# A two-block layer on one NeuronCore: u from x times g, the norm factor applied later, SSM parameters and shares in other places and types, norm sums in PSUM

## The reference, cut to what matters

```python
n = rmsnorm(h, g_mix)                    # h * rsqrt(mean(h*h) + eps) * g
z = n @ w_in                             # q, k, v of 12 heads; u (512 wide); two gates
# attention in three dilated groups of 4 heads, each with output o_g and log-denominator l_g
wts = softmax(stack(lses), axis=0)       # the "shares" of the three groups, per head and token
attn = sum(wts[..., None] * stack(outs))
y = gelu(s5_ssm(u, a_re, a_im, log_dt, b, c, d_skip))   # complex diagonal scan over u
h = h + (gate_a * (attn @ w_p) + gate_s * glu(y)) @ w_out
...                                      # norm n2, gated FFN
h = h + sigmoid(h @ w_ple_gate) * (p @ w_ple_proj)
return rmsnorm(h, g_final)               # and the second block begins with norm1 of this
# second block: adaptive norms, RG-LRU, latent attention, out projection, norm2, FFN, final norm
```

## Time and profile before

| | us |
|---|---|
| median of 3 runs | 1928.42 (1926.65 to 1929.37) |
| profiled execution | 1931.13 |
| its span, first to last instruction | 1929.3 |
| PE busy | 1859.4 (96%) |
| DVE busy | 1051.3 (54%) |
| ACT busy | 748.1 (39%) |
| POOL busy | 260.2 (13%) |

### The profile page before, as it was taken

The page is one execution under the profiler, slowest core; times in us unless marked ns, Lnnn a source line. Parts: engine busy times, 40 slices in busy tenths (PEclk is TensorE's granted clock), DMA queues, the critical chain, the costliest instruction groups (busy, mean ns, idle before and its releaser), DMA issues.

```text
span 1929.3 us, 20889 instructions
## 1 busy us (share of the span) xinstructions
PE 1859.4 (96%) x8140; PEld 1452.8 (75%) x8140; DVE 1051.3 (54%) x1562; ACT 748.1 (39%) x1181; POOL 260.2 (13%) x351
## 2 busy tenths in 40 slices
PE   5999999999999999999989999899999899999997
PEld 4888888777877888888867777666667688888885
DVE  7555454454556544553467594455545466435543
ACT  4454454442344222222343553345444244324431
POOL 7644551100000000000001140211110000000000
PEclk9999999989999999999989999999999899999998
DMA  4322222214334545552323223312104223332321
GB/s 170 115 67 88 87 67 91 88 56 142 98 124 164 178 162 187 185 184 87 126 66 115 82 67 104 125 33 72 44 22 160 86 77 89 97 99 90 96 87 56
DMA packets 64186, 199.31 MB, mean 103 GB/s; under 512 B 7124, under 2 KB 11476, under 8 KB 64088
## 3 DMA queue, kind: packets, MB, share of 16 engines
q1 hardware_dynamic: 64088, 197.97, 31.6%
HBM read 189.55 MB, written 8.39 MB: 103 GB/s over the span
## 4 chain that ended last, share of the span: by engine, by line
PE 70%; issue 20%; DVE 7%; ACT 2%; DMA 0%; POOL 0%; POOLq 0%; DVEq 0%; SPq 0%; ACTq 0%
PE bank L248 20%; PE bank L250 19%; PE bank L249 19%; PE bank L597 2%; PE bank L623 2%; PE bank L610 1%; PE bank L505 1%; DVE tile L1776 1%; DVE tiler L1307 1%; PE bank L277 1%; PE bank L317 1%; PE bank L333 1%; DVE wlo L1280 1%; ACT whi L753 1%; PE bank L395 1%
## 5 line engine op out<-in xcount | busy, mean ns | idle before, releaser
L248 PE MATMUL bank<-tiler,whi 128*128 128x512 f32 x2272 | 923.6, 407 | 15.1 <-DVE tiler L1307 5.3
L249 PE MATMUL bank<-tiler,whi 128*128 128x512 f32 x2272 | 902.7, 397 | 0.0
L250 PE MATMUL bank<-tiler,wlo 128*128 128x512 f32 x2272 | 902.5, 397 | 0.0
L753 ACT ACTIVATE whi<-raw 128x1024 fp32r<-128x1024 f32 x286 | 301.1, 1055 | 654.9 <-PE bank L250 649.3
L248 PEld LDWEIGHTS bank<-tiler,whi 128*128 128x128 f32 x2272 | 432.1, 190 | 139.1 <-issue 28.9
L250 PEld LDWEIGHTS bank<-tiler,wlo 128*128 128x128 f32 x2272 | 431.7, 190 | 101.8
L1280 DVE TENSOR_TENSOR wlo<-raw,whi 128x1024 fp32r<-128x1024 f32 x267 | 334.5, 1257 | 315.8 <-ACT whi L753 315.6
L249 PEld LDWEIGHTS bank<-tiler,whi 128*128 128x128 f32 x2272 | 432.4, 190 | 96.7 <-issue 2.9
L2016 POOL TENSOR_TENSOR stat<-stat,scl 128x4 f32<-128x4 f32 x7 | 7.9, 1130 | 1162.0 <-DVE stat L1298 725.8
L1954 DVE SCALAR_TENSOR_TENSOR tile<-bank,sm,tile 128x511 f32<-128x511 f32 x44 | 33.0, 750 | 98.4 <-ACT tile L1254 61.9
L2007 POOL TENSOR_TENSOR wlo<-raw,whi 128x1024 fp32r<-128x1024 f32 x19 | 45.5, 2397 | 257.9 <-ACT whi L753 257.9
(11 more groups left out here) (341 smaller groups left out, 1573.1 us busy)
## 6 DMA issues: line engine op xcount, KB each, us to landing
raw<-wst SPq DMA_DIRECT2D x286, 512.0 KB, 3.6
wide<-wadaT SPq DMA_DIRECT2D x48, 512.0 KB, 3.5
tile<-xT SPq DMA_DIRECT2D x16, 256.0 KB, 5.2
spare<-tile SPq DMA_DIRECT2D x16, 256.0 KB, 2.0
tile<-spare SPq DMA_DIRECT2D x16, 256.0 KB, 5.5
out<-tile SPq DMA_DIRECT2D x8, 256.0 KB, 2.0
tile<-gblk SPq DMA_DIRECT2D x5, 256.0 KB, 4.7
us<-tile SPq DMA_DIRECT2D x4, 256.0 KB, 4.7
```

Source lines behind the costliest of these rows:

```text
L248: e.matmul(bank, whi[:, o:o + 128], hi, start=start, stop=False)
L249: e.matmul(bank, whi[:, o:o + 128], lo, start=False, stop=False)
L250: e.matmul(bank, wlo[:, o:o + 128], hi, start=False, stop=stop).then_inc(*sig("blk", n))
L753: e.activation(whi[:, c % NHL * W:(c % NHL + 1) * W], raw[:, c % NRAW * W:(c % NRAW + 1) * W], ACT.Copy).then_inc(*sig("hi", c))
```

## The change

- **u from x times g.** ScalarE and VectorE make the two parts of x * g as soon as a tile of x is there (tiles `XG`), and TensorE makes all four u projections from them at once, k by k, in banks 4 to 7. The sum of n1 stands behind k = 4, the spread behind k = 5. The factor is copied to `RBS`, and `u_out` multiplies with it as u leaves the banks, on VectorE. Nine f32 matmuls on ones stand at the very start. q and k of head 0 are made side by side from the norm's operands, and the SP queue loads weight chunks between the tiles of x.
- **Order of the parameters.** The decay is made on VectorE in turn 0, the inputs in turn 1, the powers of the step in turn 2. The SSM's phases are one turn later, gelu and the parts of y too (turn 16). The root of n1 stands behind the low powers on GpSimd.
- **Shares in fp32r.** The weights are split into a high part (rows 0 to 3) and a low part (rows 32 to 35) of a tile that GpSimd has set to zero, and one fp32r matmul on 64 rows spreads their sum. The matrix that selects the row is loaded earlier and copied by ScalarE.
- **Sums in PSUM.** For r1 and r12 (PLE), n3 and the last norm the eighth square is no longer added by VectorE: `total2` sums the first seven, `total3` adds the sum over the eighth into the same four columns. `busy` puts f32 matmuls of ones of 128 columns around them. At the PLE gate ScalarE makes the squares of m - 1 ahead of the sigmoid of m.

```diff
+            def total2(name, acc, bank):
+                e.wait_ge(*at("acc", name, 6))
+                for j in range(4):
+                    e.matmul(bank[:, j:j + 1], F(acc)[:, j * 128:(j + 1) * 128], ones[:, 0:1], start=j == 0, stop=False,
+                             skip_group_check=True)
+
+            def total3(name, tmp, bank):
+                e.wait_ge(*at("sq", name, 7))
+                for j in range(4):
+                    ins = e.matmul(bank[:, j:j + 1], F(tmp)[:, j * 128:(j + 1) * 128], ones[:, 0:1], start=False, stop=True,
+                                   skip_group_check=True)
+                ins.then_inc(*sig("tot", name))
+
+            def busy(bank, n):
+                for _ in range(n):
+                    e.matmul(bank[:, 128:256], ones[:, :], ones[:, :], start=True, stop=True)
...
-            total("n1", 59, B[6])
-            spread("n1", 60, B[7])
-
-            proj2("in", 36, B[0], "in", 37, B[1], N1, "n1")
-            for j in (2, 3):
-                e.wait_ge(*at("u", j - 2))
-                proj("in", 36 + j, B[j - 2], N1)
+            for _ in range(9):
+                e.matmul(B[7][:, 0:128], ones[:, :], ones[:, :], start=True, stop=True)
+
+
+            for k in range(8):
+                e.wait_ge(*at("oplo", "xg", k))
+                for j in range(4):
+                    proj("in", 36 + j, B[4 + j], XG, [k])
+                if k == 4:
+                    total("n1", 59, B[2])
+                if k == 5:
+                    spread("n1", 60, B[3])
...
-                    e.wait_ge(*at("selp"))
+                    e.wait_ge(*at("sel_r"))
                 for g in range(3):
                     if h:
                         e.wait_ge(*at("omul", h - 1, g))
-                    e.matmul(B[2 + g], F(SELP)[0:4, h * 128:(h + 1) * 128], F(ROWS[0][g])[0:4, :], start=True,
-                             stop=True).then_inc(*sig("bc", h, g))
+                    e.matmul(B[2 + g], R(SELR)[0:64, h * 128:(h + 1) * 128], R(SHARE[g])[0:64, :], start=True, stop=True).then_inc(*sig("bc", h, g))
...
-                j, phase = (a - 2) // 3, (a - 2) % 3
+                j, phase = (a - 3) // 3, (a - 3) % 3
...
+                    if a == 0 and part < 2:
+                        if part == 0:
+                            proj2("in", 0, B[0], "in", 12, B[1], N1, "n1")
+                        continue
...
-            total("r1", 51, B[4])
-            total("r12", 52, B[5])
+            busy(B[6], 8)
+            total2("r1", 51, B[4])
+            total2("r12", 52, B[5])
+            total3("r1", 56, B[4])
+            total3("r12", 58, B[5])
+            busy(B[6], 10)
             spread("r12", 53, B[6])
             spread("r1", 54, B[7])
+            busy(B[4], 5)
...
-            total("n3", 24, B[6])
+            busy(B[7], 5)
+            total2("n3", 24, B[6])
+            total3("n3", 26, B[6])
+            busy(B[7], 8)
             spread("n3", 25, B[7])
+            busy(B[6], 9)
...
             e.activation(F(PP)[:, 0:16], col("ldt", 0, 16), ACT.Exp).then_inc(*sig("dt"))
-            for k in range(8):
-                e.wait_ge(*at("io%d" % k, 0))
-                square("n1", k, F(X_RAW[k]), 59, (60, 61))
-            e.wait_ge(*at("ang", 0))
-            e.activation(F(PP)[:, 80:96], F(PP)[:, 48:64], ACT.Sin).then_inc(*sig("sin", 0))
-            e.wait_ge(*at("ang", 1))
-            e.activation(F(PP)[:, 96:112], F(PP)[:, 64:80], ACT.Sin).then_inc(*sig("cos", 0))
-            prep(-CB)
+            prep(-2 * CB)
+            for k in range(9):
+                if k < 8:
+                    e.wait_ge(*at("io%d" % k, 0))
+                    e.activation(R(XG[k][0]), F(X_RAW[k]), ACT.Copy, scale=col("g_mix", k)).then_inc(*sig("ophi", "xg", k))
+                if k == 1:
+                    e.wait_ge(*at("ang", 0))
+                    e.activation(F(PP)[:, 80:96], F(PP)[:, 48:64], ACT.Sin).then_inc(*sig("sin", 0))
+                    e.wait_ge(*at("ang", 1))
+                    e.activation(F(PP)[:, 96:112], F(PP)[:, 64:80], ACT.Sin).then_inc(*sig("cos", 0))
+                if k in (2, 4):
+                    prep(4 * k - 2 * CB)
+                if k:
+                    square("n1", k - 1, F(X_RAW[k - 1]), 59, (60, 61))
+            prep(CB)
...
-                if a in (5, 8, 11, 14):
-                    ssm_y((a - 5) // 3)
+                if a in (6, 9, 12, 15):
+                    ssm_y((a - 6) // 3)
...
+                if a == 14:
+                    e.wait_ge(*at("selp"))
+                    e.activation(R(SELR)[0:64, :], F(SELP)[0:64, :], ACT.Copy).then_inc(*sig("sel_r"))
                 if a == 15:
                     attn_hi(0)
+                if a == 16:
                     for y in range(4):
                         e.wait_ge(*at("yt", y))
                         e.activation(F(U[y]).rearrange("p (c r) -> p r c", r=4), F(YJ[y]).rearrange("p (r c) -> p r c", r=4),
@@ -904,7 +949,6 @@
                     for y in range(4):
                         e.wait_ge(*at("gelu", y))
                         e.activation(R(Y_OP[y][0]), F(U[y]), ACT.Copy).then_inc(*sig("ophi", "y", y))
-                if a == 16:
                     attn_hi(3)
...
-                e.wait_ge(*made("pg", m))
-                if m >= 2:
-                    e.wait_ge(*at("h_pg", m - 2))
-                e.activation(F(SILU[m % 2]), B[m % 4], ACT.Sigmoid).then_inc(*sig("pg_s", m))
                 if m:
                     sums(m - 1)
+                e.wait_ge(*made("pg", m))
+                e.activation(F(SILU[m % 2]), B[m % 4], ACT.Sigmoid).then_inc(*sig("pg_s", m))
             prep(first.get(("in2", 0), 0))
...
-            e.wait_ge(*at("sq", "n1", 0))
-            for k in range(1, 8):
-                add_up("n1", k, 59, (60, 61))
-            variance("n1", B[6], 1024, ST_1)
             prep(-2 * CB)
+            for k in range(8):
+                hi, lo = XG[k]
+                e.wait_ge(*at("ophi", "xg", k))
+                e.scalar_tensor_tensor(out=R(lo), in0=F(X_RAW[k]), scalar=col("g_mix", k), in1=R(hi).bitcast(F32), op0=MUL,
+                                       op1=SUB).then_inc(*sig("oplo", "xg", k))
+                if k in (2, 4):
+                    prep(4 * k - 2 * CB)
+                if k >= 2:
+                    add_up("n1", k - 1, 59, (60, 61))
+            add_up("n1", 7, 59, (60, 61))
+            prep(CB)
+            variance("n1", B[2], 1024, ST_1)
             e.wait_ge(*at("ident"))
             diagonal("n1", ST_1, 60)
-            prep(-CB)
-            scaled("n1", 8, X_RAW, lambda k: col("g_mix", k), B[7], (62, 63, 65), N1)
+            scaled("n1", 8, X_RAW, lambda k: col("g_mix", k), B[3], (62, 63, 65), N1)
...
+            def u_out(j):
+                e.wait_ge(*made("in", 36 + j))
+                if j == 0:
+                    e.wait_ge(*at("rb_sb"))
+                e.tensor_tensor(F(U[j]).rearrange("p (r c) -> p c r", r=4), B[4 + j].rearrange("p (c r) -> p c r", r=4),
+                                F(RBS).rearrange("p (c r) -> p c r", r=4), MUL).then_inc(*sig("u", j))
+
+            u_out(0)
+            u_out(1)
+            start_of("in", 24)
...
+                then(ins)
+                e.wait_ge(*at("share0"))
+                for g in range(3):
+                    ins = e.tensor_copy(R(SHARE[g])[0:4, :], F(ROWS[0][g])[0:4, :])
+                then(ins)
+                for g in range(3):
+                    ins = e.tensor_tensor(R(SHARE[g])[32:36, :], F(ROWS[0][g])[0:4, :], R(SHARE[g])[0:4, :].bitcast(F32), SUB)
...
+                    if a == 0:
+                        u_out(2)
+                        u_out(3)
+                        decay()
...
-            e.wait_ge(*at("half"))
-            root("n1", ST_1)
...
             powers(lr, li, 4)
+            e.wait_ge(*at("half"))
+            root("n1", ST_1)
             powers(hr, hi_, 3)
...
             e.dma_start(sm[:, :], small[:, :]).then_inc(*sig("small", by=16))
+            chunks(1)
             for k in range(8):
                 e.dma_start(F(X_RAW[k]), xT[k]).then_inc(*sig("io%d" % k, 0, by=16))
+                if k in (2, 4):
+                    chunks(k // 2 + 1)
             e.dma_start(ident[:, :], consts[:, 0:128]).then_inc(*sig("ident", by=16))
```

204 lines of the change are left out of this document (108 added, 96 removed).

## The result

The changed kernel takes 1912.01 us (median of 4 runs, 1911.59 to 1913.66) against 1928.89 for the one before in the same set: ratio 0.9915, 95% interval 0.9898 to 0.9932, 16.9 us faster. The forecast was 1901, range 1891 to 1909: the direction is right, the size is not, and the time lies 3 us outside the range. The profiled execution took 1913.66, its span is 1911.9, 17.4 less than before.

A forecast was written before the change was run, and what follows sets the result against it. TensorE, busy 96% of the span, was taken as the bound. Gains 1.0 (start) + 14.5 (shares) - 1.2 (gelu) + 5 (PLE) + 5.1 (n3) + 3.1 (end) = 27.5 us off 1931.13 gave 1903.6, less 2.7: 1901, range 1891 to 1909.

The forecast's parts named there:

- The shares: Four share products per turn, fp32r instead of f32: 15.2 us saved, less a 0.7 stall for weights, gain 14.5.
- Gelu: Turn 16: gelu's work on ScalarE delays the gate of projection 53, which frees projection 55's bank: loss 1.2 us.
- The start: Up to head 0's scores: u's matmuls run while the first norm is made, GpSimd's root comes later; gain 1.0 us.
- PLE: Norm behind the PLE gate: sums in PSUM, earlier squares and a faster spread shorten the hole; gain 5 us.
- falling here leaves 3.6: PLE norm: if the clock falls during the one-column matmuls between the fillers, 3.6 us remain of a 6.3 gain.
- n3: Norm behind the second output projection: variance 2.6 us earlier, spread 1.2 shorter, 1.3 from faster matmuls behind; gain 5.1.
- End: Last norm: variance 1.9 us earlier and spread 1.2 shorter, gain 3.1; with a fallen clock 0.7.
- GpSimd runs nearly free: Rival, 17%: GpSimd's low powers are hardly hindered, factor at 28 to 30, start gains 8 to 10 us: 1893.
- shut out: Rival, 13%: dense vector work blocks GpSimd, 11 operations done by 22, the start loses 2 us: 1904.
- The fillers don't keep the clock up: Rival, 14%: the clock falls in the norms' holes despite fillers; they give 6.9 us, not 13.2: 1907.
- The shares stay slow: Rival, 4%: the fp32r share products don't speed up as meant, since half the rows count little; 6.8 us less: 1908.
- The SP queue behind u(3): Rival, 2%: writes of u waiting for u(3) hold chunk loads until the kernel is slower than before.

The follow-up runs named there:

- experiment 6: Changed kernel with the share products reading the f32 selector and f32 weights on 4 rows again, the weights' conversions left unused: 1924.71 us.
- experiment 2: Changed kernel with the four share groups one projection later on TensorE, last turn's SSM outputs ahead of the last combination on VectorE: 1906.59 us.
- experiment 8: Changed kernel with ScalarE's four copies behind the gelus and one attention copy moved behind the gate of projection 53: 1909.20 us.
- experiment 5: Changed kernel with the chunk's low part for head 0's values ahead of the sines, first two u products behind head 0's rotation: 1910.76 us.
- experiment 9: Changed kernel with ScalarE copying head 0's queries out of their bank ahead of the two sines instead of behind them: 1911.92 us.
- experiment 10: Changed kernel with the edits of experiment 5 and experiment 9 together: 1910.31 us.
- experiment 4: Changed kernel without the filler matmuls around the norms, the nine at the program's start kept: 1917.66 us.
- experiment 11: Changed kernel with n1's root amid the low powers, shares one projection later, mixed PLE fillers, chunk part and queries' copy ahead of the sines: 1897.68 us.
- experiment 12: Kernel of experiment 11 with two more chunk loads ahead of the writes of u on the SP queue: 1895.02 us.
- experiment 3: Changed kernel with four instead of eight fillers ahead of the PLE norm's sums and six between their pieces: 1911.30 us.

## Why the prediction was wrong in size

- **The shares, 14.5 forecast, 8.0 in the profile (the largest miss).** The step that failed is "the 24 matmuls of the last SSM block's output now stand ahead of the first share, 24 x 0.111 = 2.7". They stood ahead of it before as well, seventeen us earlier; timeline of TensorE, kernel before:

```profile
360.25 0.38 PE L371 MATMUL bank<-tile 128*128 128x128 f32 x2
```

  So TensorE is not later at the first share by their move: it would come at 379.8 as before, the weights were computed for 382.9, and 3.1 us of stall is the right sum, not 0.7 (2.95 measured). That stall brings a second price which I had named at 37.63 and did not add here: half clock behind it, 9.35 - 6.69 = 2.7 us (1.5 in seven other profiles with the same wait). And a share group costs 1.11, not 0.70, because each of its matmuls takes some 0.30 in place of 0.232 and the first projection matmul behind it 0.33: 1.6 over four. 14.5 - 2.3 - 2.7 - 1.6 = 7.9. The main mechanism, fp32r in place of f32, is right: experiment 6 takes it away, and experiment 2 takes away the stall and the half clock behind it.
- **Gelu, -1.2 forecast, -1.1 measured.** It is the wait at 425.52, at the gate that was named; experiment 8 removes it.
- **The start, +1.0 forecast, -0.6 in the profile.** Its parts came out nearly to the tenth: root at 33 (32.96), TensorE idle from 29, values' wait ended at 59 (59.37). The sum was short of the half clock behind that wait: from 59.37 to the scores it is 11.2 us for 36 matmuls, which take 8.4 at full clock; that is 2.9 for the clock where I added 1.6, and 0.4 comes from the later start. Five other profiles of kernels that are the same up to there have 69.21 to 70.15, so the typical gain is about 0.3. The count of GpSimd's operations rested on a poor pair of rows: the one of 1.26 us has 128 columns, which take 0.40 to 0.48 with nothing beside them, and the one of 0.21 has 16. The rule itself held: from 11.86 to 22 there are 17 operations of GpSimd and 14 of the vector engine. One cause I gave, the chunk part as the only gate, was wrong without harm: the queries' copy was the second (experiments 5, 9, 10).
- **PLE, 5 forecast, 2.0 in the profile.** Failed steps: "falling here leaves 3.6", which here left 2.0, because fillers at half clock cost double and then hold the spread by 1.1 us (I had priced them as free in every case); and "2.6 us of one-column matmuls", which are 3.5 at full clock (970.46 to 973.96 in experiment 2). In eight profiles with these fillers the hole is 11.70 (three), 13.1 to 13.2 (three) or 14.80 (two), where before it was 16.80: gains of 5.1, 3.6 and 2.0. The value of 5 is the good outcome, not the mean of 3.8. Without any filler one profile has 12.52 (experiment 4), so most of the gain here is not theirs. Timeline of TensorE in experiment 2 (11.70) and, last, in experiment 8 (13.17), where the clock fell among the ten fillers:

```profile
972.17 1.93 PE L281 MATMUL bank<-ones,tile 128*128 128x1 f32 x16
973.96 2.48 PE L287 MATMUL bank<-ones 128*128 128x128 f32 x20
...
978.13 4.11 PE L287 MATMUL bank<-ones 128*128 128x128 f32 x20
```

- **n3, 5.1 forecast, 5.1 measured.** The hole from the last output projection to `up` is 9.76 or 9.77 in all twelve profiles with its fillers. Experiment 4 shows that 3.05 of the gain is theirs.
- **End, 3.1 forecast, 2.3 measured.** Variance 1.3 nearer instead of 1.9, spread 1.0 instead of 1.2. The second sum starts 0.3 after the last square is there, and from its start to the variance it is 1.07, not 0.8.
- **Not forecast:** +2.0 between in2 and the second output projection, of which 1.6 is luck with the clock (last section), and small drifts that were not followed, -0.7 in the stretch of the heads and shares and 0.5 from there to the PLE gate. With them the misses add up: 6.5 + 1.6 + 3.0 + 0.8 - 0.1 - 2.0 + 0.7 - 0.5 = 10.0.
- **The rivals.** "GpSimd runs nearly free" and "shut out" both fall: 24 operations by 22, next to the forecast's 26. "The fillers don't keep the clock up" holds at PLE for five of the eight profiles and not at n3 or the end. "The shares stay slow" falls (experiment 2). The SP queue behind u(3) was priced right as not late in the changed kernel; it becomes a gate once head 0 starts 5 us earlier (experiments 10 to 12).

## What to carry to other kernels

When work is moved ahead of a waiting instruction, ask what stood ahead of it in the old order too: only the difference moves the arrival. Price a hole twice, once for itself and once for the half clock behind it, and fillers at half clock as well: they have to end before the next real matmul can start. At the PLE gate mixing them among the one-column products made the outcome steady at 12.15; it did not beat the good outcome of 11.70, and the time did not show it. A wait that the trace puts down to one releaser can have a second gate a microsecond or two ahead of it; open one and read the new releaser before counting the gain.

## What was not expected of the hardware

- The clock can be up behind a hole in one profile and down behind the same hole in another. At the cross attention both kernels wait 2.52 us; timeline of TensorE before:

```profile
1160.47 0.47 PE L543 MATMUL bank<-whi,tiler 128*128 128x512 f32 x1 [2.52 <-DVE tiler L1307]
...
1161.05 0.63 PE L545 MATMUL bank<-wlo,tiler 128*128 128x512 f32 x1
```

  and after:

```profile
1152.31 0.47 PE L574 MATMUL bank<-whi,tiler 128*128 128x512 f32 x1 [2.52 <-DVE tiler L1349]
...
1152.85 0.39 PE L576 MATMUL bank<-wlo,tiler 128*128 128x512 f32 x1
```

  From this matmul to the 25th it is 8.25 us there (1168.72) and 6.70 here (1159.01), both with a wait of 0.89 in them. Of the fourteen profiles ten have 8.2 to 8.3 and four 6.7; the kernels do not differ in this place. With the first share (9.35 or 8.2) and the PLE norm (11.70 to 14.80) this is what a term of one or two us can be off by in a single pair of profiles. The Trainium skill, TensorE: Matmul & The Clock Gate, Part 1, says that the same kernel starts with a different number of slow matmuls from run to run. The traces agree (the first projections of u have 12 of them at half clock in the changed kernel and 6 in experiment 3, with the same code up to there), and show it in the middle of a kernel too.
- Where the fillers stand seems to matter more than how many there are (the mixed version has two more). With eight ahead of the sums and 3.5 us of one-column matmuls behind them, the clock fell in five of eight profiles; with four ahead and six mixed in, it fell in none of four (hole 12.14 to 12.16 each time). Shown for this hole alone.
- A small GpSimd operation takes 0.50 us on average beside a dense stream of vector operations with two SBUF operands (9.89 to 22.00), and 0.25 without (23.42 to 26.14), on 16 columns there and 16 or 32 here. The Trainium skill, SBUF — State Buffer, "Who interferes with whom", calls the shared port pair an exclusive lock; the trace agrees in kind. GpSimd was not shut out for much longer than one vector operation: the longest of its own there takes 1.30 us, where a vector operation takes up to 1.23.
